# Expert weights requested while the tokens choose their experts, and the steps of neighbouring expert pairs taken in turn on TensorE

## The reference, cut to what matters

```python
combine = ...   # 512 x 32: for each token, two experts of its best group, with their weights; else 0
for e in range(N_EXPERTS):                       # 32
    he = jax.nn.silu(xt @ w_gate[e]) * (xt @ w_up[e])      # 1024 -> 256
    y = y + combine[:, e:e + 1] * (he @ w_down[e])         # 256 -> 1024
```

## Time and profile before

| | us |
|---|---|
| median of three runs | 1485.15 (1484.74 to 1487.26) |
| the profiled execution, time | 1483.6 |
| the profiled execution, span | 1481.8 |
| of it up to the first gather of the experts | 1166.2 |
| the rest: loop over pairs 0 to 13, and tail | 315.6 |

### The profile page before, as it was taken

One profiled execution on the slowest core, in us unless ns is written; L12 is line 12 of the kernel. 1 busy time (PEld: TensorE's weight loads), 2 busy tenths in 40 slices (PEclk: granted clock), 3 DMA queues, 4 the chain that ended last, 5 costly groups with the idle time before them and its releaser, 6 DMA issues. The chain is left out here.

```text
span 1481.8 us, 20028 instructions
## 1 busy us (share of the span) xinstructions
PE 1330.9 (90%) x7696; PEld 953.6 (64%) x7696; DVE 667.8 (45%) x1346; ACT 505.4 (34%) x970; POOL 575.3 (39%) x533
## 2 busy tenths in 40 slices
PE   4999999989999899898999899999998888877885
PEld 3767768778879676577889776667677633333332
DVE  5466953267713679536742414433437311111115
ACT  3312333367622433336652434544423011101112
POOL 2114686334453437953445304434324211101133
PEclk9999999999999999999999999999999899988998
DMA  8772111130032311120002311211139689998763
GB/s 339 272 291 78 44 45 55 36 122 1 2 107 78 120 50 50 57 71 16 2 26 77 114 64 58 86 51 43 45 127 344 252 341 378 390 389 357 294 242 157
DMA packets 42652, 210.06 MB, mean 142 GB/s; under 512 B 7271, under 2 KB 9703, under 8 KB 33328
## 3 DMA queue, kind: packets, MB, share of 16 engines
q1 hardware_dynamic: 34336, 195.11, 34.7%
q0 software_dynamic: 5760, 10.27, 1.9%
q10 hardware_dynamic: 2448, 3.21, 0.7%
HBM read 201.98 MB, written 17.30 MB: 148 GB/s over the span
## 5 line engine op out<-in xcount | busy, mean ns | idle before, releaser
L425 POOL TENSOR_TENSOR wlo<-raw,whi 128x1024 fp32r<-128x1024 f32 x57 | 139.3, 2446 | 106.6 <-ACT whi L413 72.6
L3258 PE MATMUL ps<-gu,XT 128*64 128x512 f32 x608 | 140.1, 614 | 14.7 <-DVE XT L3358 11.7
L853 PE MATMUL ps<-hxh,whi 128*128 128x512 f32 x304 | 130.6, 430 | 5.1 <-ACT whi L413 5.1
L853 PE MATMUL ps<-hxh,wlo 128*128 128x512 f32 x304 | 123.0, 405 | 13.6 <-POOL wlo L425 13.6
L1115 DVE SCALAR_TENSOR_TENSOR z<-glu,small,z 128x798 f32<-128x798 f32 (+1 forms) x120 | 129.1, 1126 | 0.7
L853 PE MATMUL ps<-hxl,whi 128*128 128x512 f32 x304 | 122.3, 402 | 0.0
L3258 PEld LDWEIGHTS ps<-gu,XT 128*64 128x64 f32 x608 | 51.3, 141 | 91.6 <-issue 72.6
L1618 POOL TENSOR_SCALAR P<-P,stat 128x768 f32<-128x768 f32 (+1 forms) x80 | 65.8, 825 | 84.6 <-DVE stat L1580 83.7
L3446 POOL DMA_INDIRECT ybuf<-Y,kept x17 | 16.9, 997 | 205.9 <-DVE Y L3376 101.6
L1462 PE MATMUL ps<-kT,qT 96*128 96x256 f32 (+1 forms) x432 | 91.6, 348 | 3.9 <-ACT P L1516 2.0
L1516 ACT ACTIVATE P<-ps,stat 128x768 f32<-128x768 f32 (+1 forms) x80 | 65.2, 815 | 63.0 <-DVE stat L1573 62.5
(11 more groups left out here) (839 smaller groups left out, 3184.8 us busy)
## 6 DMA issues: line engine op xcount, KB each, us to landing
gu<-in_w_gu_dram SPq DMA_DIRECT2D x32, 2048.0 KB, 9.7
raw<-in_w_in_dram SPq DMA_DIRECT2D x66, 512.0 KB, 3.3
dn<-in_w_dn_dram SPq DMA_DIRECT2D x32, 1024.0 KB, 7.9
wgate<-in_w_mod_dram SPq DMA_DIRECT2D x16, 1024.0 KB, 8.4
raw<-in_w_out_dram SPq DMA_DIRECT2D x24, 512.0 KB, 3.2
wmod<-in_w_mod_dram SPq DMA_DIRECT2D x4, 2048.0 KB, 13.3
ybuf<-zero SPq DMA_DIRECT2D x1, 4096.0 KB, 12.0
yin<-ybuf SPq DMA_DIRECT2D x4, 1024.0 KB, 10.8
```

The lines of the kernel that those rows point to most:

```text
L425: e.tensor_tensor(K.lo[i][:, :], K.raw[i % 2][:, :], K.hi[i][:, :].bitcast(F32), ALU.subtract).then_inc(*q.up("lo", i))
L853: p = e.matmul(s[0:m, o:o + n], a, K.h[l, v][x][:, k, :], start=k == 0 and part == 0 and x == 0, stop=end)
L3258: m = e.matmul(s[o, :], x[:, k, o], gu[:, k, :], start=k == 0, stop=k == KT - 1, skip_group_check=True)
```

## The change

1. **Scratch of the choice is packed closer**, so that all 13 places of weights are free of it. `h2` has two tiles in place of three, so `squares(t)` waits for the write of `h2d` of tile t-2 (before: t-3). Part of the scratch of `place` lies in the room of `xT` and `h20`. `xg0` and `xg1` are now the tiles of `row1` and `h21`, and `empty`, the two memsets of POOL, is gone.
2. **All 13 first loads go out in the choice.** The order is `gu0 gu1 dn0 dn1 gu2 dn2 dn3 dn4 dn5 gu3 gu4 gu5 gu6`; the last four wait for the last `x_out`, the others only for the end of the stage before. After that the `dn` of a pair stand one pair later in the order than they did: behind the `gu` of the next pair. `rows_in` no longer issues weights.
3. **The steps on PE are interleaved over three pairs.** In round i PE does `upward(i)`, (second group of i up to `upward`), `turned(i+1)`, `down(i-1)`, (second group of i-1: `turn_up` and `down`), `turn_up(i)`. `he` has three tiles, so that a second group keeps its own. The gather of the next pair's second group is issued before the scatter of the pair before, not behind it.

```diff
-        ("h2N", 12 * kb, 130, 139), ("xT", 8 * kb, 130, 139), ("wr", 8 * 36 * 4, 130, 139), ("rt", 16 * kb, 130, 139), ("rc", 4 * RC["all"], 130, 139),
-        ("xg", 2 * 4 * kb, 131, 149), ("xg2_", 4 * kb, 140, 149), ("XT", 4 * kb, 140, 149),
-        ("he", 3 * kb, 140, 149), ("Y", 2 * 4 * kb, 140, 199),
+        ("h2N1", 4 * kb, 130, 149), ("xT", 12 * kb, 130, 139), ("wr", 8 * 36 * 4, 130, 139), ("rt", 4 * 1056, 130, 139), ("rc", 4 * RC["all"], 130, 139),
+        ("xg2_", 4 * kb, 140, 149), ("XT", 4 * kb, 140, 149),
+        ("he", 4 * kb, 140, 149), ("Y", 2 * 4 * kb, 140, 199),
...
-    R.h2 = [sb(f"h2{i}", [128, D], F32, "h2N", 4096 * i) for i in range(3)]
+    R.h2 = [sb("h20", [128, D], F32, "xT", 8192), sb("h21", [128, D], F32, "h2N1")]
...
-    R.xg = [sb(f"xg{i}", [128, D], F32, "xg", 4096 * i) for i in range(2)]
+    R.xg = [R.row1, R.h2[1]]
...
-    empty()
     for _ in chosen[2]:
         next(chosen[3], None)
...
-        experts_load(S, 5)
+        experts_load(S, 8)
         e.dma_start(R.iota[:, :], d["iota"]).then_inc(*q.land("iota"))
...
-        for w in q(("x_out", 1, t, 0), ("x_out", 1, t, 1), *([("h2d", t - 3)] if t > 2 else after("last"))):
+        for w in q(("x_out", 1, t, 0), ("x_out", 1, t, 1), *([("h2d", t - 2)] if t > 1 else after("last"))):
...
-        wait("hi")
+        for w in q(("place", "hi"), ("h2d", 2)):
+            e.wait_ge(*w)
...
 def _expert_loads():
-    first = ["gu0", "gu1", "dn0", "dn1", "gu2", "dn2", "gu3", "dn3", "gu4", "dn4", "gu5", "dn5", "gu6"]
-    return [(w[:2], int(w[2:])) for w in first] + [(w, 2 * p + n + j) for p in range(PAIRS) for w, n in (("gu", N_GU), ("dn", N_DN))
-                                                  for j in range(2) if 2 * p + n + j < NE]
+    first = ["gu0", "gu1", "dn0", "dn1", "gu2", "dn2", "dn3", "dn4", "dn5", "gu3", "gu4", "gu5", "gu6"]
+    loads = [(w[:2], int(w[2:])) for w in first]
+    for p in range(PAIRS):
+        loads += [("gu", 2 * p + N_GU + j) for j in range(loads_of("gu", p))]
+        loads += [("dn", 2 * p - 2 + N_DN + j) for j in range(loads_of("dn", p - 1) if p else 0)]
+    return loads
...
-    if x < 3:
-        return after("last")
-    if x < 5:
-        return after("last") + [("x_out", 1, T2 - 1, 1)]
-    return after("chosen") + [("list",), *[("h2d", t) for t in range(T2)], ("first.gather", 0), ("first.gather", 1)]
+    return after("last") + [("x_out", 1, T2 - 1, 1)] * (w == "gu" and x > 2)
...
-    load(3)
     empty2()
     free.at["xg2"] = [("first.xg2",), *lists()]
     second_gather(0)
+
+    def lower(i):
+
+        job, job2 = ("first", i), ("second", i)
+        down(job, 0, None, free(("Y", 0)))
+        free.set("heT", ev("down", job, 1))
+        scattered(job, 0)
+        guarded(numbers, crowded(i), lambda: downward(job2, 1 + i % 2, 1))
+        guarded(("pool",), crowded(i), lambda: scattered(job2, 1))
+        load(loads_of("dn", i))
+    turned(("first", 0), ("xg", 0), "XT")
+    first_gather(2)
     for i in range(PAIRS - 2):
         job, job2 = ("first", i), ("second", i)
-        turned(job, ("xg", i % 2), "XT")
-        first_gather(i + 2)
-        if i:
-            second_stored(i - 1)
         upward(job, "XT", 0)
 
         def more_up():
             turned(job2, "xg2", "XT")
-            upward(job2, "XT", 1)
+            upward(job2, "XT", 1 + i % 2)
         guarded(numbers, crowded(i), more_up)
         load(loads_of("gu", i))
-        downward(job, 0, 0)
-        scattered(job, 0)
-        guarded(numbers, crowded(i), lambda: downward(job2, 1, 1))
-        guarded(("pool",), crowded(i), lambda: scattered(job2, 1))
         if i + 3 < PAIRS:
+            turned(("first", i + 1), ("xg", (i + 1) % 2), "XT")
             second_gather(i + 1)
-        if i < PAIRS - N_DN // 2 - 1:
-            load(loads_of("dn", i))
+            first_gather(i + 3)
+        if i:
+            lower(i - 1)
+            second_stored(i - 1)
+        turn_up(job, 0, free("heT"))
+        free.set(("he", 0), ev("he_turned", job))
+    lower(i)
     second_stored(i)
...
     def rows_in(end, scattered):
         for t in range(T2):
-            if t == 2:
-                experts_load(S, 2)
```

More of the change, by code:

```diff
@@ L2431, in last_buffers, with new @@
     R.xT = [sb(f"xT{i}", [128, KT, 128], F32, "xT", 4096 * i) for i in range(2)]
-    R.h2 = [sb(f"h2{i}", [128, D], F32, "h2N", 4096 * i) for i in range(3)]
+    R.h2 = [sb("h20", [128, D], F32, "xT", 8192), sb("h21", [128, D], F32, "h2N1")]
     R.ms, R.rs = K.stat[:, 48:52], K.stat[:, 56:60]
-    rt = sb("rt", [128, 4096])
-    at = [0]
-    def new(*shape, dt=None):
+    room = [sb("rt", [128, 1056]), sb("rt2", [128, 3072], F32, "xT")]
+    at = [0, 0]
+    def new(*shape, dt=None, late=0):
         n = int(np.prod(shape))
-        v = rt[:, at[0]:at[0] + n]
-        at[0] += n
-        assert at[0] <= 4096
+        v = room[late][:, at[late]:at[late] + n]
+        at[late] += n
+        assert at[late] <= room[late].shape[1]
         if dt:
@@ L2454, in last_buffers @@
     R.M, R.A, R.w12 = new(2, T2, NE), new(T2, NE), new(2, T2)
[L2455 to L2460, removed]
+    R.cmp, R.nb, R.past = new(NE, 4, late=1), new(NE, late=1), new(NE, late=1)
+    R.many, R.p16 = new(NE, late=1), new(PAIRS, late=1)
+    R.ctl, R.eq = new(2 + MORE, late=1), new(MORE, NE, late=1)
+    R.G, R.H = new(T2, NE, late=1), new(T2, NE, late=1)
+    R.slot = new(2 * T2, late=1)
+    R.whole, R.low, R.hi = (new(2 * T2, dt=U32, late=1) for _ in range(3))
     n = 2 * T2
-    R.ones_at, R.here, R.what = new(n, 128), new(n, G_ALL), new(n, 3, G_ALL)
+    R.ones_at, R.here, R.what = new(n, 128, late=1), new(n, G_ALL, late=1), new(n, 3, G_ALL, late=1)
     g = G_ALL
@@ L2485, in last_walk @@
 def last_walk(S, loads=nothing, more_loads=nothing, weights=nothing, out=nothing, squares=nothing, turn=nothing, logits=nothing, rows=nothing,
-              choose=blank, empty=nothing, place=nothing):
+              choose=blank, place=nothing):
     chosen = {}
@@ L2644, in rows @@
             e.wait_ge(*w)
-        e.activation(R.h2[t % 3][:, :], C.xN[:, t, :], ACT.Copy, scale=R.rs[:, t:t + 1]).then_inc(*q.up("row", t))
+        e.activation(R.h2[t % 2][:, :], C.xN[:, t, :], ACT.Copy, scale=R.rs[:, t:t + 1]).then_inc(*q.up("row", t))
     def choose(t):
@@ L2864, in rows @@
     def rows(t):
-        h2 = R.h2[t % 3]
+        h2 = R.h2[t % 2]
         for w in q(("row", t), ("row1",)):
@@ L2871, in rows @@
         e.dma_start(K.h2d[128 * t:128 * t + 128, :], h2[:, :]).then_inc(*q.land_as(f"h2d{t}", "h2d", t))
[L2873 to L2877, removed]
     def place(_):
@@ L2885, in place, with _expert_loads @@
         e.tensor_tensor(R.what[:, :, 1, :], R.here, over(ids[:, :, 1], G_ALL), ALU.mult).then_inc(*q.up("place.what1"))
[L2886 to L2898 removed]
+    last_walk(S, squares=squares, rows=rows, place=place)
 def loads_of(w, p):
     return max(0, min(2, NE - 2 * p - dict(gu=N_GU, dn=N_DN)[w]))
+def _expert_loads():
+    first = ["gu0", "gu1", "dn0", "dn1", "gu2", "dn2", "dn3", "dn4", "dn5", "gu3", "gu4", "gu5", "gu6"]
[4 more added lines that the diff above has]
+    return loads
+EXPERT_LOADS = _expert_loads()
 def weight_place(K, w, x):
@@ L2939, in experts_buffers @@
     E.Y = [sb(f"Y{i}", [128, D], F32, "Y", 4096 * i) for i in range(2)]
-    E.he = [sb(f"he{j}", [128, 256], F32, "he", 1024 * j) for j in range(2)]
-    E.heT = sb("heT", [128, 2, 128], F32, "he", 2048)
+    E.he = [sb(f"he{j}", [128, 256], F32, "he", 1024 * j) for j in range(3)]
+    E.heT = sb("heT", [128, 2, 128], F32, "he", 3072)
     last = PAIRS - 3
@@ L3069, in experts_walk @@
     for i in range(2):
-        free.at["xg", i] = [("place.xg", i), *lists()]
+        free.at["xg", i] = [("row_scaled", T2 - 1), *lists()]
         first_gather(i)
-    load(3)
     empty2()
```

9 lines of the change are left out of this document (4 added, 5 removed).

## The result

| | before | after |
|---|---|---|
| median of 4 runs each, one chip | 1486.20 us (1484.74 to 1487.75) | 1470.02 us (1468.34 to 1471.47) |
| ratio, 95% interval | | 0.9891 [0.9878, 0.9905] |
| the profiled execution: time, span | 1483.6, 1481.8 | 1470.25, 1468.4 |

Faster by 16 us, where 27 were forecast: 1470.02 stands just above the upper end of the range. The picture of the trace is the one that was forecast, and its sizes are not.

A forecast was written before the change was run, and what follows sets the result against it. PE bounds the loop; the change gains PE 44.1 us, of which memory, the next bound, takes 17 back. The loop ends 27.2 us earlier, so 1485.15 - 27.2 = 1458 us, range 1440 to 1470 for 8 in 10.

The forecast's parts named there:

- What bounds what: Pair loop: PE bounds it before; after the change weights do, with PE standing 12.8 us for `dn27` before `down(13)`.
- rival (b): Pair loop: PE loses its clock whenever it stands for weights and falls behind, up to 1563 us; chance 0.04.
- (a): Weight stream: memory is faster, 2.62 us a MiB, and PE stays the bound, giving 1441 us; chance 0.13.
- (d): PE's loop: the new order waits for PSUM banks, so holes stay in every round, 1466 to 1470 us; chance 0.03.
- (c): Choice and stream: choice loses 4 us more, 66 MiB run at 3.05 us each (+10), 1468 to 1472 us; chance 0.15.
- The early loads worth nothing: Loads during the choice: 5 MiB moved earlier gain nothing afterwards, since `gu7` still waits for pair 0's up products, about 1190 us.
- The choice: Choice of experts: memsets gone -1.9 us, `squares(3)` waiting for `h2d` +3.1, net +1.2, bounds -1.7 and +2.5.
- The path of PE: Pair loop on PE alone: holes covered, 12.2 us a round instead of 14.38, loop end at 1386.3 instead of 1430.4.
- From there 2.90 us a MiB: Weight stream from `gu8`'s landing at 1204.1: unbroken at the earlier kernel's rate, so `dn27` lands at 1395.5.
- The clock behind the stand: After PE's stand for `dn27`: at half rate `down(13)` takes 7.3 us instead of 3.65, the tail's first transposes 0.4 more.
- The tail: After the pair loop: same work in the same order, nothing added, a tail of 51 us.
- within cover: Scatter that must land before `Y` is free again: 10.7 us against a round of 12.2, costed at nothing.

The follow-up runs named there:

- e1_late3: The changed kernel, but `gu4`, `gu5` and `gu6` wait for the end of the choice and the first two gathers: 1468.89 us, 0.9886 of the kernel before.
- e2_half: The changed kernel, but only half of each `gu` from `gu7` on is loaded, products unchanged in size: 1447.79 us, 0.9726 of the kernel before.
- e3_quarter: The changed kernel, but mid-loop first-group gathers and scatters move 256 numbers of each row instead of 1024: 1453.99 us, 0.9763 of the kernel before.

## Why the prediction came out as it did

**What bounds what: right.** PE was the bound, memory became it. PE stands for `dn` before the last `down` and nowhere long before (0.94 us at 1287, 1.7 at 1319, 3.06 and 1.70 before `down(12)`). Not rival (b): the clock stays at 1.00 over the nine blocks. It falls twice at their end. The first time is behind the stands of 3.06 and 1.70 us before and in `down(12)`: it is 0.50 from 1392 to 1394, the fourteen matmuls take 4.99 us in place of 3.65, and from 1396 on it is back at 1.00. The second time is in the long stand. Not (a): there is a stand. Not (d): 12.0 us a round, no hole. What came is the forecast with the sizes of (c), which had 1468 to 1472; but (c) laid 4 us on the choice, and they were not there.

**The early loads worth nothing: right,** by e1_late3. The forecast that `gu7` leaves when pair 0's up products end is right to the tenth of a us: 1186.81 + 7.09 = 1193.9, issue at 1194.0. The second gather's wait of 1.07 us went. The absolute time, "within 2 us of 1190", did not come, as the whole stage began late. And one sign of being wrong did, on a small scale: "no place is full in this stretch" does not hold for `gu9`, which waited 1.2 us until PE was done with pair 1, at 1202.7. It cost nothing that the trace shows, since `gu8` was still on its way (DMA share 0.96 from 1202 to 1204). A slip of the text, 14 MiB behind `gu0` and 4 more, should be 13 and 5, as its own "three loads (5 MiB)" has it; it was costed at nothing.

**The choice: +1.2 forecast, +0.5 measured.** The stage began 4.5 us late (the load of `row1` at 1113.34, before at 1108.82), and PE's first transposes of pair 0 at 1176.14 against 1171.14: 5.0, so 0.5 in the choice. That is less than the profiles differ among themselves: this stretch took 62.3 and 63.1 us in the two of the kernel before, 62.8 and 62.9 in those of the changed one. The memsets are gone, and with them DVE's operation of 2.13 us; two stretched ones beside POOL's row products stay (1.69 and 2.37 us, before 1.68 and 2.37). But it was `squares(2)`, for which I allowed 0.5 us, and not `squares(3)` that waited. ACT's timeline:

```profile
1138.55 1.06 ACT L2641 ACTIVATE h<-xN 128x1024 f32<-128x1024 f32 x1 [2.98 <-DMA h2d<-h]
...
1143.67 1.06 ACT L2641 ACTIVATE h<-xN 128x1024 f32<-128x1024 f32 x1 [1.02 <-DVE xN L2216]
```

`squares(3)` came after it in ACT's queue, and by then `h2d` of tile 1 was there. The wait of 2.98 us is near the 3.1 that I had, but that is luck: it is another wait, for another write. I looked only at the one and not at what an earlier wait of the same kind does to it.

**The path of PE: right.** 12.2 forecast, 12.0 measured. The loop by PE alone ended at 1389.1 in e2_half against 1386.3, with first transposes at 1176.3 against the forecast's 1171.1 + 1.2 = 1172.3: 212.8 us against 214.0.

**The term that was mis-sized is the stream.** "From there 2.90 us a MiB": `dn27` was due at 1395.5, and the matmuls that wait for it start at 1411.2. Of these 15.7 us, 3.9 are `gu7` leaving at 1194.0 and not 1190.1, and -1.2 are the first four MiB, there after 12.8 us in place of 14.0: `gu10` left at 1206.8, behind a wait of 3.7 us for `gu8` to land. The remaining 13.0 are 66 MiB at 204.4 / 66 = 3.10 us and not 2.90, the same rate as over the nine blocks in between (3.09). So the step of the prediction that failed is this one: the stream of the kernel before was taken over at 2.90 us a MiB, and it ran at 3.10. I took the rate from a window of the kernel before, and with it the number of gathers and scatters beside each block. The change shortens PE's round from 14.38 to 12.0 us, and each round brings its own rows: by e3_quarter some 0.2 to 0.7 us a block, 2 to 8 us of the 13. What is left is the difference from one execution to the next, whose cause stays open: the 17.40 us a block that I started from is the fastest of three with the order of before, and the 18.55 measured is above the mean of 18.2. The bounds of 2.82 to 2.98 around 2.90 had a single profile behind them; the eight with the changed order have 2.94 to 3.11. Rival (c) had named both the packing of the rows and a price, 3.05. The 425 GB/s of the Trainium skill (DMA: Bandwidth & Descriptors, section Bandwidth) were reached over no long window of the stream in any of the profiles: the nine blocks have 374.

**The clock behind the stand:** 7.3 + 0.4 us forecast for `down(13)` and the transposes; the fourteen matmuls took 5.69 and the transposes 1.06, so 2.0 us less. PE did two of the matmuls at 0.50 before it stood again, and the window of the fourteen has 0.64.

**The tail: right,** 51.5 us against 51.4, and partly by luck. Its first wait, 0.74 us, was short only because `down(13)` was so late: the scatter of pair 12 had been issued at 1398.72, and the read-outs of `down(13)` at 1414.90 and 1416.91 no longer waited for it. I costed this scatter "within cover" by 10.7 us against a round of 12.2. After pair 12 there is no `upward` and so no round: with the weights there in time, it is the next in line, 4 to 9 us.

**A second step failed, the edit that was costed at nothing without a word:** the list of tiles. The diff changes sizes and lifetimes in it, and the addresses move; that is 3.3 us in a stretch of the kernel that the prediction never looked at, and most of the 4.5 us by which the last stage began late.

So the profiled span: 1454.6 forecast, + 15.7 for the weights, - 2.0 for the clock, + 0.1 for the tail, 1468.4 measured. Of the 15.7, 13.0 are the rate and 3.9 the late start. That is 13.8 us more; the medians are 12.0 apart, as this profiled run lies 0.2 us above its median and that of before lay 1.6 below.

## What to carry to other kernels

When a change makes one engine's round shorter, what that engine brings to the shared resource in each round comes closer together: take the bandwidth left for the stream at the new round, and its spread from more than one execution. Where two loads or stores are covered by "one round", look at the last round by itself, since it has none behind it. And an edit to a planned memory layout is an edit to the whole kernel: compare the event times of the untouched stages first, before the difference is sought in the changed one.

## What the runs showed that I had not expected

Addresses alone decided over PE's clock at one place: behind a wait of 3.15 us it stayed at 1.00, behind one of 3.22 to 3.24 us at the same place it was near 0.50 for some 6 us, and the stretch took 3.3 us more; the 13 profiles part cleanly by their addresses, five and eight. A scatter of a pair's rows beside the weight stream took 12 us from issue until DVE could go on, where the median of the kernel before was 8.9. And the rate of one and the same stream differed by 5% between profiles of kernels whose loads were all but the same, 368 to 388 GB/s.
